# Expert rounds of 64, 32 and 32 places, the branch and the halves moved, and the norm's rows loaded late

## What is computed

```python
h = x * (1 + scale2) + shift2
scores = sigmoid(h @ router_w)             # 256 x 64
# the best 4 of 8 groups, then the best 8 of their experts, weights normed and times 2.5
y_e = (silu(xb @ w_gate[e]) * (xb @ w_up[e])) @ w_down[e]   # tokens xb of expert e; 1024 -> 256 -> 1024
x = layer_norm(ALPHA * x + gate2 * (routed + shared), ln2_g[l], ln2_b[l])
```

## Time and profile before

| | us |
|---|---|
| profiled execution, whole | 3601.73 |
| its span | 3599.9 |
| median of three runs | 3595.91 |
| TensorE busy | 3083.4 (86%) |
| VectorE busy | 1134.1 (32%) |
| ScalarE busy | 606.5 (17%) |
| data moved | 703.48 MB, mean 195 GB/s |

### The profile page before, as it was taken

The page is one execution under the profiler, slowest core; times in us unless marked ns, Lnnn a source line. Parts: engine busy times, 40 slices in busy tenths (PEclk is TensorE's granted clock), DMA queues, the critical chain, the costliest instruction groups (busy, mean ns, idle before and its releaser), DMA issues.

```text
span 3599.9 us, 68634 instructions
## 1 busy us (share of the span) xinstructions
PE 3083.4 (86%) x29288; PEld 2289.9 (64%) x29288; DVE 1134.1 (32%) x2239; ACT 606.5 (17%) x1172; POOL 216.6 (6%) x188
## 2 busy tenths in 40 slices
PE   7987867895898866799599999999997889786999
PEld 5766534563767644455385644468877778785888
DVE  1235222232234422222354521001144562445100
ACT  0111111110110111111132310000023322332100
POOL 0000000000000000000000000000014401431000
PEclk9998988897898987899799999999989999998999
DMA  7554898998573679899713621234430023000342
GB/s 280 204 227 174 319 387 332 390 415 347 166 292 149 251 307 358 336 415 415 284 47 135 212 75 70 78 119 142 151 112 16 4 81 113 8 4 2 141 153 104
DMA packets 116307, 703.48 MB, mean 195 GB/s; under 512 B 11328, under 2 KB 11504, under 8 KB 49888
## 3 DMA queue, kind: packets, MB, share of 16 engines
q1 hardware_dynamic: 112224, 685.47, 49.4%
q0 software_dynamic: 3712, 12.61, 1.1%
HBM read 696.98 MB, written 1.05 MB: 194 GB/s over the span
## 4 chain that ended last, share of the span: by engine, by line
PE 43%; DVE 4%; ACT 2%; issue 1%; POOL 0%; DVEq 0%; ACTq 0%; POOLq 0%
PE ps L1586 9%; PE ps L1599 9%; PE ps L2229 7%; PE ps L217 5%; PE ps L1936 4%; DVE arena L150 2%; PE ps L557 1%; ACT arena L133 1%; PE ps L584 1%; PE ps L355 1%; PE ps L2611 1%; PE ps L2234 1%; PE ps L2241 1%; DVE arena L154 1%; PE ps L572 1%
## 5 line engine op out<-in xcount | busy, mean ns | idle before, releaser
L1157 PE MATMUL ps<-arena 128*32 128x256 f32 (+2 forms) x4096 | 425.7, 421 | 166.7 <-DMA arena<-in_w_gate 142.7
L217 PE MATMUL ps<-arena 128*128 128x256 f32 (+1 forms) x2208 | 533.9, 405 | 24.4 <-ACT arena L133 11.2
L217 PEld LDWEIGHTS ps<-arena 128*128 128x128 f32 x2208 | 431.8, 197 | 124.6 <-issue 47.3
L133 ACT ACTIVATE arena<-ps 128x512 f32<-128x512 f32 (+1 forms) x488 | 251.2, 515 | 1457.5 <-PE ps L1586 296.1
L1157 PEld LDWEIGHTS ps<-arena 128*32 128x32 f32 (+2 forms) x4096 | 273.9, 139 | 322.6 <-issue 243.4
L2229 PE MATMUL ps<-arena 64*64 64x64 f32 x10496 | 308.9, 225 | 60.9 <-issue 22.5
L1586 PE MATMUL ps<-arena 128*128 128x512 f32 (+1 forms) x1024 | 336.6, 492 | 10.0 <-DVE arena L159 10.0
L2229 PEld LDWEIGHTS ps<-arena 64*64 64x64 f32 x10496 | 295.5, 140 | 74.9 <-issue 38.5
L1599 PE MATMUL ps<-arena 128*128 128x256 f32 x1536 | 332.0, 379 | 0.0
L1599 PEld LDWEIGHTS ps<-arena 128*128 128x128 f32 x1536 | 291.8, 190 | 40.1 <-issue 0.5
L150 DVE TENSOR_TENSOR arena<-arena,ps 128x512 f32<-128x512 f32 (+1 forms) x264 | 158.1, 599 | 464.9 <-PE ps L2229 245.1
(11 more groups left out here) (200 smaller groups left out, 2387.6 us busy)
## 6 DMA issues: line engine op xcount, KB each, us to landing
arena<-in_w_gate SPq DMA_DIRECT2D x128, 1024.0 KB, 12.5
arena<-in_w_up SPq DMA_DIRECT2D x128, 1024.0 KB, 13.4
arena<-in_w_down SPq DMA_DIRECT2D x128, 1024.0 KB, 10.8
arena<-in_mlp SPq DMA_DIRECT2D x80, 1024.0 KB, 4.7
arena<-in_w_ada SPq DMA_DIRECT2D x48, 1024.0 KB, 6.9
arena<-in_ada SPq DMA_DIRECT2D x48, 1024.0 KB, 4.9
arena<-in_w_in SPq DMA_DIRECT2D x30, 1024.0 KB, 5.6
arena<-in_w_rkv SPq DMA_DIRECT2D x20, 1024.0 KB, 4.8
```

The costliest lines, as they stand in the source:

```text
L133: self.e.activation(out, in_, func, bias=bias, scale=scale, **more).then_inc(*self.done(key))
L217: ins = pe.matmul(out, a, b, start=start and i == 0, stop=stop and i == len(pairs) - 1)
L1157: ins = pe.matmul(psum.of["gu", l, new][w * ab:w * ab + w, i_ * 256:i_ * 256 + 256], xe[:, k, new % 2 * 128 + w * ab:new % 2 * 128 + w * a ...
```

## The change

- **The plan.** NR stays 26; widths are now 2 2, then 3 3 3 3 1 3 3 1 3 3 1 3 3 1, 3 3 3 3, 2 2 2 2, 3 3. A round of 3 has places of 64, 32 and 32 tokens and is computed in four column groups of 32, the first two on the same expert's weights (`column_groups`). There are 16 rounds of 3, 6 of 2 and 4 of 1. How many places there are of each size is as before (4 of 128, 28 of 64, 32 of 32).
- **The branch** stands directly behind the up products on TensorE, ahead of `add(0)`, the gathers and `add(1)`; on ScalarE and VectorE ahead of the gathers' copies and of `choose`.
- **The halves** XH and XL are made right after VectorE's share of the turned copies, before it waits for the scores. The flags, the maxima, the masks and `choose(1)` come behind `choose(0)`; the flags and maxima ahead of the first gathers' copies, the masks and `choose(1)` behind them. The subtraction of 1 from the place numbers is gone (the column numbers start at 1).
- **choose** works round by round and group by group: two operations for each run of equal places, over both halves of the tokens.
- **w_down and ws_down** lie in memory as rows of 8 KB per partition, as gate and up do.
- **The norm's rows** are loaded behind the up products of round 23 into the memory of XE[1], the gathered columns of the odd pairs; the 8 KB they had become a 13th slot (NEXTRA = 8).

```diff
-NEXTRA = 7
+NEXTRA = 8
-PLAN = (2, 1, 4, 2, 4, 1, 4, 2, 2, 2, 2, 2, 4)
+FORMS = {1: (128,), 2: (64, 64), 3: (64, 32, 32)}
+PLAN = (2, 2) + (3, 3, 3, 3, 1, 3, 3, 1, 3, 3, 1, 3, 3, 1) + (3, 3, 3, 3) + (2, 2, 2, 2) + (3, 3)
+BY_FORM = sorted(range(NR), key=lambda r: (r > 1, PLAN[r], r))
+SEAT = [BY_FORM.index(r) for r in range(NR)]
...
+        def column_groups(r, ws):
+
+            w = min(FORMS[PLAN[r]])
+            return [(o, o + w, a) for (o0, o1), a in zip(columns_of(r), ws) for o in range(o0, o1, w)]
...
+                self.last_odd = max(r for r in range(NR) if r // 2 % 2)
+                self.lg, self.lb = xe1[:, 0:1024], xe1[:, 1024:2048]
...
             pool.dma_start(E.order, D["order"]).then_inc(*tables["order"](("order", l), 16))
+            pool.wait_ge(*at["up", l, E.last_odd])
             pool.dma_start(E.lg, D["ln2_g"][l].partition_broadcast(128)).then_inc(*tables["moe"](None, 16))
             pool.dma_start(E.lb, D["ln2_b"][l].partition_broadcast(128)).then_inc(*tables["moe"](("moe", l), 16))
...
                             if name == "w_down":
-                                load(sp, (name, l, e), ("yd", l, new, 1), src, 2)
+                                load(sp, (name, l, e), ("yd", l, new, 1), src)
...
                     for k in range(8):
-                        for ab in range(WIDTH[new]):
-                            ins = pe.matmul(psum.of["gu", l, new][w * ab:w * ab + w, i_ * 256:i_ * 256 + 256],
...
+                        for o, o_, w in column_groups(new, ws):
+                            ins = pe.matmul(psum.of["gu", l, new][o:o_, i_ * 256:i_ * 256 + 256],
...
                 if new is not None:
                     hidden(1, "w_up").then_inc(*made(("up", l, new)))
-                def add(nh):
...
-                if p >= 0:
-                    add(0)
-                for nh in range(2):
-                    if ks:
-                        gather(Q, ks[2 * nh], 2 + nh)
-                if p >= 0:
-                    add(1)
-
                 def block():
...
                     over(pe, over_pe, l, new, block)
+                def add(nh):
...
+                if p >= 0:
+                    add(0)
+                for nh in range(2):
+                    if ks:
+                        gather(Q, ks[2 * nh], 2 + nh)
+                if p >= 0:
+                    add(1)
...
             turned_out(dve, do, 0, E.hT, l, 1)
+            xk = XS[:, :].rearrange("p (t d k) -> p t k d", t=2, k=8)
+            high, low = (x_.rearrange("p (t k d) -> p t k d", t=2, k=8) for x_ in (E.XH, E.XL))
+            for t in range(2):
+                do.cp(high[:, t], xk[:, t])
+                do.tt(low[:, t], xk[:, t], f32(high[:, t]), ALU.subtract)
             dve.wait_ge(*at["scores out", l])
...
             def choose(Q):
...
+                for r in (2 * Q, 2 * Q + 1):
+                    for w, same in groupby(zip(places_of(r), columns_of(r)), lambda c: c[1][1] - c[1][0]):
...
+                        do.tt(sa, bc(bc(E.iota[:, 0:w], 1, n), 1, 2), bc(E.sv[:, :, e:e + n], 3, w), ALU.is_equal)
+                        do.tt(sw, f32(sa), bc(E.gtv[:, :, e:e + n], 3, w), ALU.mult, ("chosen", l, Q) if ends else None)
...
             dve.wait_ge(*at["tri"])
             choose(0)
-            choose(1)
+            do.cp(flags[:, 64 + l * 64:128 + l * 64], gt[:, 0:64])
...
+            do.cp(flags[:, l * 32:l * 32 + NR], gt[:, 64:64 + NR], ("flags", l))
             for k in (2, 3, 6, 7):
                 gather(0, k)
+            do.tt(E.grv[:, :, 0:64], E.sv, bc(E.caps, 1, 2), ALU.is_gt)
+            do.tt(E.grv[:, :, 0:64], E.grv[:, :, 0:64], E.gtv[:, :, 0:64], ALU.mult)
+            choose(1)
...
-    A["w_down"] = I["w_down"]
+    A["w_down"] = np.ascontiguousarray(I["w_down"].reshape(2, 64, 2, 128, 1024).transpose(0, 1, 3, 2, 4)).reshape(2, 64, 128, 2048)
```

More of the change, by code:

```diff
@@ L1186, in moe_pe @@
                     hidden(1, "w_up").then_inc(*made(("up", l, new)))
-                def add(nh):
[L1188 to L1191, removed]
-                                            y_[:, nh * 512:nh * 512 + 512], start=False, stop=p == NR - 1 and y_ is E.YL)
-                    ins.then_inc(*made(("added", l, p, nh)))
-                if p >= 0:
-                    add(0)
-                for nh in range(2):
-                    if ks:
-                        gather(Q, ks[2 * nh], 2 + nh)
-                if p >= 0:
-                    add(1)
                 def block():
@@ L1238, in moe_pe @@
                     over(pe, over_pe, l, new, block)
+                def add(nh):
+                    reach(pe, *at["yl", l, p, nh])
+                    for t in range(2):
+                        for y_ in (E.YH, E.YL):
+                            ins = pe.matmul(psum.tiles[ACC + t * 2 + nh][:, :], E.ST[p % 2][:, t * 128:t * 128 + 128],
+                                            y_[:, nh * 512:nh * 512 + 512], start=False, stop=p == NR - 1 and y_ is E.YL)
+                    ins.then_inc(*made(("added", l, p, nh)))
+                if p >= 0:
[5 more added lines that the diff above has]
+                    add(1)
                 psum.among = (p % 2,)
@@ L1294, in moe_act @@
                     over(act, over_act, l, new, block)
+                for k in ks[0:2]:
+                    gather(Q, k)
             ln_act(act, do, ("moe", l))
@@ L1357, in moe_dve @@
             do.tt(gt[:, 0:64], b[:, 128:192], E.caps, ALU.is_gt, ("counts", l))
-            do.cp(flags[:, 64 + l * 64:128 + l * 64], gt[:, 0:64])
-            for n, same in groupby(range(NR), lambda r: WIDTH[r]):
-                same = list(same)
-                o, r = BASE[same[0]], len(same)
-                do.red(gt[:, 64 + same[0]:64 + same[0] + r], gt[:, o:o + n * r].rearrange("p (r e) -> p r e", e=n), ALU.max)
-            do.cp(flags[:, l * 32:l * 32 + NR], gt[:, 64:64 + NR], ("flags", l))
@@ L1427, in moe_dve @@
                     over(dve, over_dve, l, new, block)
+                for k in ks[2:4]:
+                    gather(Q, k)
+                if p >= 0 and p % 2 == 0 and p < NR - 4:
+                    choose((p + 4) // 2)
                 for _ in range(n):
@@ L2863, in layout @@
     order = np.zeros((128, 353), np.float32)
-    later = sorted(range(len(FIRST), 64), key=lambda e: (WIDTH[next(r for r in range(NR) if e in places_of(r))], e))
+    later = sorted(range(len(FIRST), 64), key=lambda e: (-CAPS[e], e))
     order[:, list(range(len(FIRST))) + later] = np.arange(64)
@@ L2868, in layout @@
     order[:, 64:128] = bias
-    order[:, 128:192] = [128 // WIDTH[r] + 0.5 for r in range(NR) for _ in places_of(r)]
-    order[:, 192:320] = np.arange(128)
+    order[:, 128:192] = np.array(CAPS) + 0.5
+    order[:, 192:320] = np.arange(128) + 1
     order[0:64, 320], order[0:64, 321:353] = bias, np.arange(64)[:, None]
```

78 lines of the change are left out of this document (32 added, 46 removed).

## The result

| us | before | after |
|---|---|---|
| median of the runs | 3595.69 (3588.16 to 3597.12) | 3496.75 (3483.86 to 3503.48) |
| profiled execution, whole / its span | 3601.73 / 3599.9 | 3495.75 / 3493.6 |

The ratio is 0.9725 [0.9694, 0.9756]: 99 us faster. The forecast was 3471, in a range from 3440 to 3522.

The account below looks back on a forecast made before the run. Expert stages bound by weight transfer, with holes worth 58 and 65 us; 54.5 + 62.9 + 21.8 - 8 - 6 = 125 us off the profiled 3601.7 gives 3476.5, on the median's scale 3471 us, range 3440 to 3522.

Parts of the forecast that it names:

- Full rate between the first release and the last landing: Expert stages' weight stream: 414 GB/s throughout, freeing 54.5 and 62.9 us in the two layers if no hole is left.
- A reserve of at least 4 us: no hole: Two three-wide rounds in a row, 13 slots: slots free after 3.7 to 11.3 us, needed at 15.5 us.
- The slow branch: TensorE's branch in three-wide rounds: half slow, each 5.7 us idle plus some 1.6 from lower clock; 4 us a layer charged.
- the tail: End of each layer's expert stage: last add now behind the branch, 0.5 us later if quick, 6 if slow; 3 a layer.
- the first rival: Every three-wide branch is slow: 16 to 17 us a layer and 3 us more tail, 38 in all, 3509 us; chance 0.20.
- (1, 3, 3): A one-wide and two three-wide rounds: TensorE 44.7 us, 52.0 with half the branches slow, against 53.1 us of DMA.
- The signs: Expected in the profile: above 405 GB/s, first gate 9.5 us sooner, thinly spread weight waits, three-wide branches 1 or 7 us.
- The head: Before and in round 0: start 9.5 us sooner, branch ahead of gathers wins 1.4 us; 10.9 us per layer, 21.8 in all.
- The sooner branch: Two- and one-wide rounds: slots come free some 2 us sooner where DMA engines are full anyway; worth nothing.
- 8 KB runs: Down weights in 8 KB instead of 4 KB runs: nothing taken; upper bound 1%, 4 us a layer.
- norm rows: Norm rows loaded behind round 23's up: 3 to 4 us at full rate, hidden by two three-wide rounds of 45 us.
- The other rivals: Holes remain, 3530 us (0.10); only the head won, 3574 (0.05); slower, TensorE bound at lower clock, 3714 (0.04).

Follow-up runs that it names:

- without branches: The changed kernel with one branch per layer and engine ahead of the rounds and the loop written twice, with and without overflow blocks: 3466.4 us.
- the variant with the short block: The changed kernel with only the first expert's overflow block of each round coded on all three engines: 3455.5 us, 0.9614 of the kernel before.
- The block cut in two: The changed kernel with TensorE's overflow branch of a three-wide round made two, over the first two experts and over the third: 3502.4 us, 0.9746.

## Why the prediction was right, and where it fell short

**Full rate between the first release and the last landing: right.** Predicted 466.5 and 476.1 us if no hole is left. With quick branches it is 465.4 and 473.8, without branches 463.7 and 471.6. The model of bytes over the rate of a full stretch holds, and so does the count of slots as long as branches are quick: then no slot came late. Where they took 3 to 7 us, the step "A reserve of at least 4 us: no hole" was wrong: slots came late for 18.6 us.

**The slow branch: the mis-sized term.** I took half of the three-wide branches as slow; it was 24 of 32. I charged 4 us a layer for it and 3 for the tail, 14 in all. Against the variant with the short block, issue to landing is 14.2 and 16.6 us longer and the tail 4.7 and 2.5: 38 us, 24 more than charged. With quick branches the stages came out some 8 us better than the working has them, mostly by the shorter tail. That leaves the 16 us between the 125 forecast and the 109 saved in the stages; the medians lack 26, and the rest lies within the scatter outside the stages.

Both the share and the path were wrong. By the prediction's own scale, an estimate, the share is the larger fault: the first rival, all slow, gives 3509, and three quarters slow lies halfway between that and 3471, at 3490, so 19 of the 26 us. As for the path, the working charged a slow branch only where (1, 3, 3) doesn't pass 53.1 us. The runs show two more ways in which it costs. Slots come late for 18.6 us where with quick branches none does, and between the holes the stream is slower (2.60 us per tile against 2.56). The lower clock was also undercharged: behind the pause that ends at 407.38 us the add takes 0.9 us more and the gathers 1.5 (3.62 for 2.07 us at full clock), where I had 1.6 for both.

**The reason for three places was weak.** "Half of them" was the middle between two rows. The rule beside it, of the Trainium skill (Runtime: NRT & Kernel Launch, section Instruction fetch mechanics), pointed to "mostly outside", and it was the better guide. The block cut in two shows the same from the other side: my picture of a distance that one jump passes is wrong. What was right in it is that the cost hangs on bringing in a packet of instructions, which all 25 slow branches waited for.

**The signs.** The rate was to be above 405 GB/s in every stretch; it was 401 and 400 over the stages, and 374 and 382 in two slices. Round 0's gate was to come 9.5 us sooner; counted from XS turned it came 8.1 us sooner in layer 0 and 11.5 in layer 1. Waits for gate weights were not in pieces of 7 to 14 us, but 7 of at most 5.8. The branches were of both kinds.

**The head: right.** Predicted 10.9 us a layer; from XS turned to the first issue behind round 0 it went from 65.8 to 56.2 and from 65.3 to 53.0, together 21.9 for 21.8. The cover held with 1.45 us left, where I had worked out 1.7.

**The sooner branch: nothing, right for this plan.** With the branch behind the adds the kernel isn't slower (3489.1 against 3496.8 us). In the old plan with 12 slots, head, branch and rows together give 43 us against before. The head has 19 of these up to round 0's gate; the stretches became 27 us shorter, and that this is the sooner branch, since a four-wide round holds all slots until it is over, is argued and wasn't run by itself.

**8 KB runs, three-wide columns, norm rows: right.** Runs make no difference. The 64 matmuls take 3.66 us for 3.67. The rows are loaded behind round 23's up and nobody waits:

```profile
782.50 0.53 POOL L1029 DMA_DIRECT2D arena<-in_ln_g  x1 [486.81 <-PE ps L1173]
```

**The tail: predicted 3 us a layer, was 1.9 and 0.3.** With quick branches it is shorter than before by 2.8 and 2.2 us, where I had added 0.5. The end of layer 0 in after, a slow branch again:

```profile
823.17 3.66 PE L1173 MATMUL ps<-arena 128*32 128x256 f32 x64 [0.34 <-DMA arena<-in_w_up]
...
830.57 3.75 PE L1241 MATMUL ps<-rounded 128*128 128x512 f32 x8 [3.73 <-PEq L993]
...
835.26 3.99 PE L1196 MATMUL ps<-arena 128*32 128x512 f32 x32 [0.52 <-DVE arena L184]
```

**The other rivals.** Holes worth half of the 117 us didn't stay, the rate wasn't held by the memory (419 GB/s), and TensorE never became the bound: its granted clock was 0.93 in both stretches, above the 0.88 and 0.87 of before.

**The account of the gain.** Against the medians: head, branch and rows 43 us, the slot 38, the plan 19, in this order; in another, the plan 50 and the slot 6. What I expected at the experiments, that the plan carries it, was wrong.

## What to carry to other kernels

Where a stage is bound by transfers, take its time as bytes over the rate of a stretch that is full, and then ask of each conditional in the loop what it costs when it isn't taken: time it in the trace, from flag to semaphore, for the longest block. If the blocks are rare, take one decision ahead of the loop and write the loop twice; it gave 30 us here, with the rest of the loop as it was. And measure overlapping cures in both orders, for a buffer more and a better order of rounds were worth 38 and 50 us alone and 57 together.

## What the runs showed of the hardware

In after, with the DMA engines full, a branch of TensorE's queue over code that isn't run took 0.9 to 1.6 us (26 of 52), 3.1 to 7.3 us (25), and once 2.3. Over one expert's block it was always quick (1.3 at most), over three experts' slow in 24 of 32. In every slow one a 16.4 KB packet of instructions ended 1.4 to 1.6 us before the queue went on. Cut in two jumps, one of the two was slow in 22 of 32 rounds and never both. The far jump ahead of round 0, with the DMA engines busy for 0.59 and 0.48 of it, took 5.6 and 4.6 us from load to first raise, again with such a packet that ended 1.5 us before the first raise, and the raises behind it came 0.15 us apart (16 from 343.2 to 345.5). Behind a pause of 5.60 us, at a granted clock of 0.50, an add took 2.05 us and the one 5 us later, at 0.98, 1.16, so a pause costs some 0.9 us more in that add alone than the pause itself. The core took 413 to 415 GB/s over stretches of 464 to 474 us.
